# Expert up weights joined into loads of 4 MB, with rows and columns dealt out by fours

## What is computed

```python
def run_block(args):              # one block of tokens of one of 32 experts, 4 experts a token
    tok_b, gate_b, e = args
    xb = hf[tok_b]                                  # hf: (256, 1024)
    gu = xb @ w_up[e] + b_up[e]                     # w_up[e]: (1024, 2048), 8 MB
    x_glu, x_lin = jnp.split(gu, 2, axis=-1)
    x_glu = jnp.minimum(x_glu, SWIGLU_LIMIT)
    x_lin = jnp.clip(x_lin, -SWIGLU_LIMIT, SWIGLU_LIMIT)
    act = x_glu * jax.nn.sigmoid(SWIGLU_ALPHA * x_glu) * (x_lin + 1.0)
    y = act @ w_down[e] + b_down[e]                 # w_down[e]: (1024, 1024), 4 MB
    return y * gate_b[:, None]
# then: out = zeros.at[slot_tok].add(ys)
# after the mixture:
x = x + sigmoid(h @ ple_gate_w) * (p @ ple_proj_w)  # h = rms_norm(x); ple_gate_w: (1024, 1024)
```

## Time and profile before

| | |
|---|---|
| runs | 1157.25, 1157.29, 1157.68 us |
| profiled execution | 1156.24 us |
| its span | 1154.4 us, granted clock 0.994 |
| TensorE busy | 1104.0 us, 96% |
| VectorE, ScalarE, GpSimd busy | 408.7, 232.9, 21.1 us |
| HBM read | 446.05 MB, 387 GB/s over the span |
| queue of SyncE | 444.44 MB, 93.3% of 16 engines |
| chain that ended last | TensorE 56%, DMA 39% |

### The profile page before, as it was taken

The page is one execution under the profiler, slowest core; times in us unless marked ns, Lnnn a source line. Parts: engine busy times, 40 slices in busy tenths (PEclk is TensorE's granted clock), DMA queues, the critical chain, the costliest instruction groups (busy, mean ns, idle before and its releaser), DMA issues.

```text
span 1154.4 us, 14307 instructions
## 1 busy us (share of the span) xinstructions
PE 1104.0 (96%) x5779; PEld 529.0 (46%) x5779; DVE 408.7 (35%) x703; ACT 232.9 (20%) x333; POOL 21.1 (2%) x34
## 2 busy tenths in 40 slices
PE   9999999999999999999999999999999999999997
PEld 8899998433333333333333333333333333333336
DVE  6899997322222221221212222222222222222237
ACT  5645454301100100000100010100000001111027
POOL 2100000000000000000000000000000000000011
PEclk9999999999999999999999999999999999999999
DMA  9985579899999999999999999999999999999991
GB/s 281 354 281 170 183 293 376 310 391 428 427 427 429 427 429 428 428 429 430 427 429 428 428 430 428 428 428 429 429 429 427 428 427 428 427 429 427 426 398 58
DMA packets 57969, 447.65 MB, mean 388 GB/s; under 512 B 4179, under 2 KB 24907, under 8 KB 32747
## 3 DMA queue, kind: packets, MB, share of 16 engines
q1 hardware_dynamic: 56932, 444.44, 93.3%
q0 software_dynamic: 672, 1.99, 0.6%
q10 hardware_dynamic: 327, 0.69, 0.2%
HBM read 446.05 MB, written 1.05 MB: 387 GB/s over the span
## 4 chain that ended last, share of the span: by engine, by line
PE 56%; DMA 39%; ACT 2%; DVE 1%; SPq 1%; issue 1%; POOL 0%; DVEq 0%; ACTq 0%; POOLq 0%
DMA down_ring<-in_expert_w_down_dram 19%; PE ps L2010 17%; DMA up_ring<-in_expert_w_up_dram 16%; PE ps L2051 14%; PE ps L1745 5%; PE ps L2064 3%; PE ps L1935 3%; PE ps L1755 3%; DMA up_ring<-in_ple_gate_w_dram 2%; PE ps L1811 2%; DMA up_ring<-in_w_in_dram 1%; PE ps L1837 1%; PE ps L1816 1%; ACT hT L965 1%; PE ps L2165 1%
## 5 line engine op out<-in xcount | busy, mean ns | idle before, releaser
L2010 PE MATMUL ps<-up_ring,hT 128*64 128x512 f32 x2040 | 447.8, 593 | 11.0 <-DMA up_ring<-in_expert_w_up_dram 10.5
L2010 PEld LDWEIGHTS ps<-up_ring,hT 128*64 128x64 f32 x2040 | 150.1, 137 | 299.5 <-issue 273.5
L2051 PE MATMUL ps<-down_ring,hT 128*64 128x512 f32 x992 | 231.1, 608 | 24.4 <-DMA down_ring<-in_expert_w_down_dram 17.8
L1502 DVE TENSOR_SCALAR extra<-ps 128x512 f32<-128x512 f32 x32 | 22.1, 692 | 506.9 <-PE ps L2021 506.9
L1488 DVE TENSOR_TENSOR x_sb<-x_sb,ps 128x1024 f32<-128x1024 f32 x64 | 78.2, 1221 | 185.3 <-PE ps L2064 178.7
L2051 PEld LDWEIGHTS ps<-down_ring,hT 128*64 128x64 f32 x992 | 68.5, 139 | 163.6 <-issue 140.9
L961 ACT ACTIVATE work<-ps 128x512 f32<-128x512 f32 x31 | 18.5, 597 | 377.2 <-PE ps L2021 377.2
L1745 PE MATMUL ps<-h_hi,w_hi 128*128 128x256 f32 x304 | 74.3, 285 | 2.1 <-ACT up_ring L834 2.1
L1745 PE MATMUL ps<-h_lo,w_hi 128*128 128x256 f32 x304 | 73.8, 283 | 0.0
L2064 PE MATMUL ps<-hT,extra 64*128 64x512 f32 x256 | 72.0, 640 | 0.8 <-DVE hT L1537 0.8
L472 DVE TENSOR_TENSOR w_lo<-up_ring,w_hi 128x2048 fp32r<-128x2048 f32 x28 | 64.0, 2289 | 6.9 <-ACT w_hi L766 6.8
(11 more groups left out here) (312 smaller groups left out, 808.4 us busy)
## 6 DMA issues: line engine op xcount, KB each, us to landing
up_ring<-in_expert_w_up_dram SPq DMA_DIRECT2D x125, 2048.0 KB, 27.0
down_ring<-in_expert_w_down_dram SPq DMA_DIRECT2D x63, 2048.0 KB, 21.5
up_ring<-in_w_in_dram SPq DMA_DIRECT2D x21, 1024.0 KB, 6.8
up_ring<-in_branch_w_dram SPq DMA_DIRECT2D x6, 1024.0 KB, 5.1
up_ring<-in_expert_w_up_dram SPq DMA_DIRECT2D x5, 1024.0 KB, 11.3
up_ring<-in_w_out_dram SPq DMA_DIRECT2D x4, 1024.0 KB, 6.9
up_ring<-in_ple_gate_w_dram SPq DMA_DIRECT2D x4, 1024.0 KB, 25.1
down_ring<-in_expert_w_down_dram SPq DMA_DIRECT2D x2, 1024.0 KB, 21.0
```

Source lines behind the costliest of these rows:

```text
L1502: nc.vector.tensor_scalar(lin, ps[:, LIN, :], 1.0 + LIMIT, 1.0 - LIMIT, ALU.min, ALU.max).then_inc(lin_ready, 1)
L2010: ins = nc.tensor.matmul(ps[64 * g:64 * g + 64, GLU + side, :], xe[:, j, k % 4, k // 4, :], w[:, D * side + 512 * g:D * side + 512 * (g + 1)],
L2051: last = nc.tensor.matmul(ps[64 * g:64 * g + 64, Y, :], actT[:, r, c, :], down_units[:, c, D * r + 512 * g:D * r + 512 * (g + 1)], start=( ...
```

## The change

For experts 4 to 29, two up units are loaded by one DMA of 4 MB, with one run of 32 KB on each partition: four adjacent rows of w_up (`load_up_pair`, `refill_up_pairs`). Such a load waits until both units of the pair are used, and raises one semaphore, that of the pair's first unit. TensorE waits for it before the first unit of a pair and not before the second. Experts 0 to 3, 30 and 31 keep single loads, now of two of those four rows, so that the runs of one load lie 32 KB apart.

The gather reads xs with a step of four floats, and moe_gain follows. The columns are shared out by fours: g = 0 computes columns 0 to 3, 8 to 11 and so on, g = 1 the others, so the up products and the bias products read four adjacent columns and skip four (`gated_columns`). A partition then has eight adjacent rows of w_down, four in each unit: a down load keeps its runs of 16 KB, now 32 KB apart. In the order of loads, experts 17 to 21 have both units of their first pair ahead of the down load before them, where it was one unit (for 17, units had alternated).

```diff
+JOINED_UP = range(4, N_EXP - 2)
             def load_up(j, c, e):
-                rows = expert_w_up[0, bass.ds(e, 1)].rearrange("a (c p r) n -> p (a c) (r n)", p=P, r=UP_ROWS)
-                sp.dma_start(up_units[:, UP_UNITS * j + c, :], rows[:, c, :]
+                rows = expert_w_up[0, bass.ds(e, 1)].rearrange("a (h p k r) n -> p (a h) k (r n)", p=P, k=2, r=UP_ROWS)
+                sp.dma_start(up_units[:, UP_UNITS * j + c, :], rows[:, c // 2, c % 2, :]
                              ).then_inc(up_loaded[UP_UNITS * j + c], 16)
 
+            def load_up_pair(j, h, e):
+                first = UP_UNITS * j + 2 * h
+                rows = expert_w_up[0, bass.ds(e, 1)].rearrange("a (h p r) n -> p (a h) (r n)", p=P, r=2 * UP_ROWS)
+                sp.dma_start(up_units[:, first:first + 2, :].rearrange("p s b -> p (s b)"), rows[:, h, :]
+                             ).then_inc(up_loaded[first], 16)
+
             def load_down(c, e):
-                rows = expert_w_down[0, bass.ds(e, 1)].rearrange("a (c p r) n -> p (a c) (r n)", p=P, r=DOWN_ROWS)
+                rows = expert_w_down[0, bass.ds(e, 1)].rearrange("a (p c r) n -> p (a c) (r n)", p=P, r=DOWN_ROWS)
...
+            def refill_up_pairs(q, j, e, halves=range(2)):
+
+                for h in halves:
+                    sp.wait_ge(up_used, UP_UNITS * (q - 2) + 2 * h + 2)
+                    load_up_pair(j, h, e)
...
             with sp.Fori(2, EARLY_LOADS // 2) as i:
                 for j in range(2):
-                    refill_up(2 * i + j, j, 2 * i + j)
+                    refill_up_pairs(2 * i + j, j, 2 * i + j)
                     refill_down(2 * i + j - 1, 2 * i + j - 1)
             e = EARLY_LOADS
-            refill_up(e, 0, e)
+            refill_up_pairs(e, 0, e)
             refill_down(e - 1, e - 1)
-            for c in range(DOWN_UNITS):
-                refill_up(e + 1, 1, e + 1, [c])
-                refill_down(e, e, [c])
-            refill_up(e + 1, 1, e + 1, range(DOWN_UNITS, UP_UNITS))
-            for q in range(e + 1, e + 5):
-                refill_up(q + 1, (q + 1) % 2, q + 1, [0])
+            for q in range(e, e + 5):
+                refill_up_pairs(q + 1, (q + 1) % 2, q + 1, [0])
                 refill_down(q, q)
-                refill_up(q + 1, (q + 1) % 2, q + 1, range(1, UP_UNITS))
+                refill_up_pairs(q + 1, (q + 1) % 2, q + 1, [1])
             refill_down(e + 5, e + 5)
             with sp.Fori(EARLY_LOADS // 2 + 3, N_EXP // 2 - 1) as i:
                 for j in range(2):
-                    refill_up(2 * i + j, j, 2 * i + j)
+                    refill_up_pairs(2 * i + j, j, 2 * i + j)
                     refill_down(2 * i + j, 2 * i + j)
...
-                        rows = xs[:, a, 512 * g:512 * (g + 1)].rearrange("p (c n r) -> p c r n", c=2, r=UP_ROWS)
+                        rows = xs[:, a, 512 * g:512 * (g + 1)].rearrange("p (n r) -> p r n", r=2 * UP_ROWS)
...
+            def gated_columns(w, side, g):
+
+                return w[:, D * side:D * (side + 1)].rearrange("p (n g r) -> p g n r", g=2, r=DOWN_ROWS)[:, g]
...
-                    else:
+                    elif c % 2 == 0:
                         pe.wait_ge(up_loaded[UP_UNITS * j + c], 16 * turn + 16)
+                    elif not joined(q, JOINED_UP):
+                        pe.wait_ge(up_loaded[UP_UNITS * j + c], 16 * single_loads(q, 2, JOINED_UP))
...
                                                        xe[:, j, k % 4, k // 4, :],
-                                                       w[:, D * side + 512 * g:D * side + 512 * (g + 1)],
+                                                       gated_columns(w, side, g),
```

More of the change, by code:

```diff
@@ L562, in _ @@
             load_down(0, 0)
-            early_rows = expert_w_up[0, EARLY_EXPERT].rearrange("(c p r) n -> p c r n", p=P, r=UP_ROWS)
+            early_rows = expert_w_up[0, EARLY_EXPERT].rearrange("(h p r) n -> p h r n", p=P, r=2 * UP_ROWS)
             sp.dma_start(early_row, early_rows[:, 0, 0, :]).then_inc(single_rows_loaded, 16)
-            rows = expert_w_up[0, 0].rearrange("(c p r) n -> p c r n", p=P, r=UP_ROWS)
+            rows = expert_w_up[0, 0].rearrange("(h p r) n -> p h r n", p=P, r=2 * UP_ROWS)
             for r in range(UP_ROWS):
@@ L568, in _ @@
                 sp.wait_ge(w_used, OUT_UNIT0 + 1 + r)
-                sp.dma_start(up_ring[:, RAW_SLOT + r, :], rows[:, 2, r, :]).then_inc(landed, 16)
+                sp.dma_start(up_ring[:, RAW_SLOT + r, :], rows[:, 1, r, :]).then_inc(landed, 16)
             sp.dma_start(b_rest[:, :].rearrange("p (c n) -> p c n", c=2),
@@ L590, in load_last_rows @@
                 c = UP_UNITS - 1
-                rows = expert_w_up[0, e].rearrange("(c p r) n -> p c r n", p=P, r=UP_ROWS)
+                rows = expert_w_up[0, e].rearrange("(h p k r) n -> p h k r n", p=P, k=2, r=UP_ROWS)
                 for r in range(UP_ROWS):
                     landed = single_rows_loaded if r == 0 else up_loaded[UP_UNITS * j + c]
-                    sp.dma_start(up_ring[:, 2 * (UP_UNITS * j + c) + r, :], rows[:, c, r, :]).then_inc(landed, 16)
+                    sp.dma_start(up_ring[:, 2 * (UP_UNITS * j + c) + r, :], rows[:, 1, 1, r, :]).then_inc(landed, 16)
             def load_gate():
@@ L605, in load_last_halves @@
                 c, n = DOWN_UNITS - 1, UNIT
-                rows = expert_w_down[0, e].rearrange("(c p r) n -> p c (r n)", p=P, r=DOWN_ROWS)
+                rows = expert_w_down[0, e].rearrange("(p c r) n -> p c (r n)", p=P, r=DOWN_ROWS)
                 for half in range(2):
@@ L655, in _ @@
                             q = N_EXP * r + 2 * i + j
-                            refill_up(q, j, 2 * i + j)
+                            refill_up_pairs(q, j, 2 * i + j)
                             refill_down(q, 2 * i + j)
@@ L701, in _ @@
             pool.dma_start(rb[:, :], on_all(router_b[0])).then_inc(mats_loaded, 16)
-            pool.dma_start(moe_gain[:, :].rearrange("p (c r) -> p c r", r=UP_ROWS),
-                           moe_norm[0].rearrange("(c p r) -> p c r", p=P, r=UP_ROWS)).then_inc(mats_loaded, 16)
+            pool.dma_start(moe_gain[:, :].rearrange("p (h r) -> p h r", h=2),
+                           moe_norm[0].rearrange("(h p r) -> p h r", h=2, p=P)).then_inc(mats_loaded, 16)
             pool.wait_ge(sgu_loaded, 32)
@@ L1962, in _ @@
                     for g in range(2):
-                        rows = xs[:, a, 512 * g + 256 * c:512 * g + 256 * (c + 1)].rearrange("p (n r) -> p r n", r=UP_ROWS)
+                        rows = xs[:, a, 512 * g:512 * (g + 1)].rearrange("p (n c r) -> p c r n", c=2, r=UP_ROWS)[:, c]
                         last = nc.tensor.matmul(ps[64 * g:64 * g + 64, (GATHER, ACTT)[c], 0:256], select[:, 0, a, :],
@@ L1979, in biases_to_tokens, with joined, single_loads @@
                 last.then_inc(comb_done, 1)
+            def gated_columns(w, side, g):
+                return w[:, D * side:D * (side + 1)].rearrange("p (n g r) -> p g n r", g=2, r=DOWN_ROWS)[:, g]
+            def joined(q, loads):
+                return not isinstance(q, int) or q in loads
+            def single_loads(q, step, loads):
+                return sum(e not in loads for e in range(q % step, q + 1, step))
             def up(q, j, turn, first=False, part=None, last=False, early_result=False):
@@ L2003, in up @@
                         if by_row and r == 1:
-                            pe.wait_ge(up_loaded[UP_UNITS * j + c], 16 * turn + 16)
+                            pe.wait_ge(up_loaded[UP_UNITS * j + c], 16 * single_loads(q, 2, JOINED_UP))
                         if first and c == 0 and r == 1:
@@ L2021, in up @@
                         ins = nc.tensor.matmul(ps[64 * g:64 * g + 64, GLU + side, :], pick_bias[:, :],
-                                               b_parts[:, D * side + 512 * g:D * side + 512 * (g + 1)],
+                                               gated_columns(b_parts, side, g),
                                                start=False, stop=True)
```

## The result

The changed kernel takes 1181.78 us (median of six runs; the kernel before 1157.49 us beside it), a ratio of 1.0203 with a 95% interval of 1.0187 to 1.022: some 24 us, 2%, slower. One of the six runs took 1646.29 us at a granted clock of 0.654 and is left out of the ratio; the median of the other five is 1180.76 us. The forecast was 1156.1 us, 1152.5 to 1161. The profiled execution has a span of 1179.0 us where it was 1154.4.

A forecast was written before the change was run, and what follows sets the result against it. The stream of expert weights was taken as the bound, TensorE 8% behind. The end was to move -1.9 us without a clock fall, -0.4 with one; the middle gave 1157.29 - 1.2 = 1156.1 us, range 1152.5 to 1161.

The forecast's parts named there:

- the gather's: Gather's read of xs at a step of four: some 40 ns more an instruction, +0.16 us a gather.
- my upper bound of 0.7: Most a gather could lose, in us, from weight loads at a step of four against adjacent ones, ratio 1.44.
- rule of four pairs: In a gather two instructions run side by side, so the added time of one counts 4 times.
- rival (c): Strided reads turn TensorE into the bound: 1174 us at a halved rate, about 1158.0 at +0.7 us; chance 0.18.
- the deciding point: Added time a gather from which TensorE decides throughout: +1.1 us, from 34 us of slack in 31 gathers.
- Runs of 32 KB: Up loads of experts 4 to 29: 52 joined loads save 88 ns each, 4.6 us of stream.
- Down rows 32 KB apart: Down loads and single up loads: same bytes and packets, nothing taken, about 1 us either way allowed.
- Coarser release: A pair's first half is asked for 3.5 us later; the queue covers it, so the DMA engines have no gap.
- Coarser landing: TensorE waits once, at an expert's second pair; at the end this takes back 3.1 of 4.6 us.
- Columns by fours: Up products reading four adjacent floats, then skipping four: nothing taken, 593 ns kept; otherwise 1.5 us on the end's way.
- The clock: TensorE's granted clock may fall after the new 2.1 us waits: gain on its way 1.2 us, or -0.3 us.
- Rival (a): The whole stream gain reaches the end by the gate's way: 4.6 us less, 1152.7 us; chance 0.20.
- Rival (b): Nothing is saved in the stream of loads, and the end comes later: 1160.0 us; chance 0.12.

The follow-up runs named there:

- runs with pairs: The kernel before, with a gather that reads two adjacent floats of every four: 1159.16 us, a single run.
- the run with adjacent reads: The changed kernel, but ScalarE writes xs in the gather's order, so both gathers read adjacent floats: 1156.83 us, ratio 0.9988.
- the run with both helps: The changed kernel, both gathers reading adjacent floats and writing spread over PSUM, the projection moved to experts 22 to 25: 1155.04 us, ratio 0.9967.

## Why the prediction was wrong

**The step that failed is the gather's.** The term was +0.16 us a gather; it is 1.8 us, eleven times as much and two and a half times my upper bound of 0.7. The rest of that step held: by its own rule of four pairs, 1074 for 612 ns makes 4 x 462 ns = 1.85 us. What was wrong is the price of the read, +40 ns an instruction where it is +462, and with it the claim that the stream stays the bound. The prediction's own sign for that, a mean of the gather above 900 ns, came up. The working was an extrapolation without a basis: the 19 ns between a step of two and adjacent floats were put down to the columns lying over 4 KB in place of 2 KB. They do not: in either form the 512 columns of one g are the same 2 KB of xs, only read in another order. The runs with pairs and with a step of eight show the kind of law, a threshold and not a slope. And the upper bound, taken from weight loads at 208 for 144 ns, was no bound: it is the price of a weight load, and the moving operand paid 1.75 times where the weight load paid 1.44. No row of before had a moving operand at a step of four, so the range had to take in the halved rate that rival (c) priced, which is the other side of the 34 us of slack.

**The rival was named and priced, and given too little.** (c) had the mechanism, the deciding point (+1.1 us a gather) and 1174 us at a halved rate (+1.65 us, measured 1.83), with a chance of 0.04. The sum by its own terms: the slack of 33.9 us (1093.81 - 325.04 - 27 x 26.93 - 4 x 1.94, the last from experts of 28.87 us) stands against 31 x (28.76 - 26.93) = 56.7 us for the later gathers, 1.8 us for the first one, which the rival left out, and 0.7 us by which the mixer ended later in this execution (the first gathers of the kernel before and the runs start anywhere from 211.6 to 215.5 us): 25.3 us later, measured 25.2 at the start of expert 31, less 0.68 us of idle time that goes away at the gate. The deciding point is bracketed: 0.9 us a gather costs 1.5 us in all, 1.8 us a gather costs 20 or more. The rule of the Trainium skill in "SBUF — State Buffer", Door 1 (The DMA port swizzle), two accesses to a line of 16 bytes, is what these reads obey: step of two and pairs 612 ns, step of four 1074, step of eight 1093, four adjacent floats of eight 593. Only the 20 ns between 612 ns and the 592 of adjacent floats are outside it.

**The other steps,** read in the run with adjacent reads, where they can be seen:
- Runs of 32 KB go through whole: the packets show it, and the period is 29.22 us for 29.20. From 320 to 1080 us, with 48 of the 52 joined loads, the stream gains about 3.3 us where 48 x 88 ns = 4.2 us were forecast; what takes the rest is not shown.
- Down rows 32 KB apart: no run has them alone. A cost of more than some 0.02 us an expert would show in the period, if a joined load saves what was forecast.
- Coarser release: no sign of a gap in the slices of the runs with a fast gather. In the changed kernel itself the ninth and tenth slices have 367 and 407 GB/s for 391 and 428. The kernel before with the gather's step alone has 364 and 423, with single loads: so the ninth is TensorE's late release, and only the tenth leaves room for the pairs.
- Coarser landing: the single wait of 2.1 us came as described. That it takes back part of the gain at the end looks right in size (1.4 us net of the kernel before, 1.2 forecast), but that is partly luck: the stream gained less than forecast, and the start lost 1.1 us that the forecast didn't have. Nor is it the pair of expert 29 alone: the run with single loads there gained 0.2 us. Behind the pair, a fall of the clock and 28.87 us of TensorE's work in each of the experts with the projection hold the end almost as late.
- Columns by fours: right, 593 ns before and after, and 388 for 379 ns in the bias products.
- The clock: falls came after some waits of 2.1 us, as after some of 2.4 us, and not after others.
- Rival (a) needed TensorE out of the way; the run with both helps comes near it, 3.5 us for 4.6.
- Rival (b) falls: joined loads do save time.

## What to carry to other kernels

A change of layout for one engine's sake has to be followed to every reader: here 52 better loads were worth 3 us, and re-ordered reads in 32 gathers cost 58 us of an engine that had 34 to spare. When a cost is unknown and a near-critical engine pays it, divide the engine's slack by the number of times first, and ask what could exceed the quotient. Where an order is needed and only one side of the product can be strided cheaply, try the other side, here the write to PSUM.

## What the runs showed of the hardware

- A float32 moving operand (the one that streams through TensorE, here 512 columns) with neighbours 16 or 32 bytes apart halves the product's rate: 1074 ns (step of four) and 1093 ns (step of eight) an instruction for 592 ns. A gather of eight takes 3.7 us for 1.9. With two neighbours within 16 bytes it is 612 ns, with four, even if the next four are skipped, 593 ns.
- A float32 product that writes PSUM with 512 bytes between neighbouring columns takes 592 ns, the same as one that writes adjacent columns.
- ScalarE's copy of 1024 floats on each partition, read with a step of four and written adjacent, took 2124 ns for 1136 ns. With a step of two (the kernel before with its own order) it took 1210 ns: again little at 8 bytes between neighbours and much at 16.
- A DMA run of 32 KB on a partition passes at a slightly higher rate than two of 16 KB: 29.22 us for an expert's 12 MB with 8 MB of it in such runs, 29.38 us without. The order of the down rows changed with it.
